# A relative-bias table kept in DRAM: one reversed row per head in place of 128 copies, and the reads that follow from it

## What is computed

```
def dsa_attention(q, k, v, iq, ik, iw, rel_bias):
    ...
        sc = jax.nn.relu(jnp.einsum('bthd,bsd->bths', iqb, ik))
        score = jnp.einsum('bths,bth->bts', sc, iwb).astype(jnp.float32)
        ...
        _, idx = lax.top_k(score, topk)
        ...
        bucket = t5_bucket(jnp.maximum(t[None, :, None] - idx, 0))
        bias = rel_bias[bucket].astype(jnp.float32).transpose(0, 1, 3, 2)
        logits = jnp.einsum('bthd,btkhd->bthk', qb, k_sel).astype(jnp.float32) * (dh ** -0.5) + bias
```

## Time and profile before

| | us |
|---|---|
| median of 3 runs | 1810.75 |
| lowest and highest run | 1805.5 and 1813.46 |
| span of the profiled execution | 1806.1 |
| PE busy | 1744.1 (97%) |
| DVE busy | 1028.2 (57%) |
| ACT busy | 854.6 (47%) |
| POOL busy | 628.9 (35%) |
| mean granted TensorE clock | 0.968 |

### The profile page before, as it was taken

The page is one execution under the profiler, slowest core; times in us unless marked ns, Lnnn a source line. Parts: engine busy times, 40 slices in busy tenths (PEclk is TensorE's granted clock), DMA queues, the critical chain, the costliest instruction groups (busy, mean ns, idle before and its releaser), DMA issues.

```text
span 1806.1 us, 23068 instructions
## 1 busy us (share of the span) xinstructions
PE 1744.1 (97%) x8072; PEld 1370.1 (76%) x8091; DVE 1028.2 (57%) x1633; ACT 854.6 (47%) x1366; POOL 628.9 (35%) x275
## 2 busy tenths in 40 slices
PE   7999999999999999999998999999999999999999
PEld 5548877767688778866667887888878788888887
DVE  4129937866733677677778325555547555556300
ACT  4222347665524455576664336676673343444220
POOL 3204421132244234443434432222124334444442
PEclk9759999999999899999999998999999999999999
DMA  6503222121323223311111321111113322333331
GB/s 180 126 12 94 94 88 59 42 81 48 127 86 111 69 72 104 95 57 47 48 47 49 111 74 47 48 47 47 48 48 105 94 82 93 93 100 97 95 103 59
DMA packets 40850, 141.16 MB, mean 78 GB/s; under 512 B 4664, under 2 KB 5144, under 8 KB 40632
## 3 DMA queue, kind: packets, MB, share of 16 engines
q1 hardware_dynamic: 37600, 131.96, 23.4%
q10 hardware_dynamic: 3160, 7.99, 2.1%
HBM read 135.21 MB, written 4.72 MB: 77 GB/s over the span
## 4 chain that ended last, share of the span: by engine, by line
PE 77%; DVE 11%; ACT 6%; issue 4%; DMA 1%; POOL 1%; DVEq 0%; POOLq 0%; ACTq 0%; SPq 0%
PE bank L673 15%; PE bank L675 14%; PE bank L674 14%; PE bank L1222 4%; PE bank L1223 4%; PE bank L1224 4%; PE bank L764 2%; PE bank L1117 2%; PE bank L724 1%; PE bank L726 1%; PE bank L725 1%; DMA w_raw<-weights 1%; PE bank L793 1%; PE bank L1136 1%; PE bank L1048 1%
## 5 line engine op out<-in xcount | busy, mean ns | idle before, releaser
L563 POOL TENSOR_TENSOR w_lo<-w_raw,w_hi 128x1024 fp32r<-128x1024 f32 x243 | 591.3, 2435 | 1138.8 <-ACT w_hi L1240 994.3
L673 PE MATMUL bank<-u_hi,w_hi 128*128 128x512 f32 x800 | 344.6, 431 | 3.2 <-DVE taps L2176 3.2
L675 PE MATMUL bank<-u_hi,w_lo 128*128 128x512 f32 x800 | 319.4, 399 | 0.0
L674 PE MATMUL bank<-u_lo,w_hi 128*128 128x512 f32 x800 | 318.9, 399 | 0.0
L1240 ACT ACTIVATE w_hi<-w_raw 128x1024 fp32r<-128x1024 f32 x199 | 209.3, 1056 | 227.1 <-PE bank L675 176.3
L673 PEld LDWEIGHTS bank<-u_hi,w_hi 128*128 128x128 f32 x800 | 153.7, 192 | 81.9 <-issue 49.4
L675 PEld LDWEIGHTS bank<-u_hi,w_lo 128*128 128x128 f32 x800 | 154.1, 193 | 33.9
L674 PEld LDWEIGHTS bank<-u_lo,w_hi 128*128 128x128 f32 x800 | 154.7, 193 | 28.5 <-issue 3.4
L1224 PE MATMUL bank<-u_hi,w_lo 128*128 128x512 f32 x320 | 124.6, 389 | 0.0
L1222 PE MATMUL bank<-u_hi,w_hi 128*128 128x512 f32 x320 | 124.6, 389 | 0.0
L1223 PE MATMUL bank<-u_lo,w_hi 128*128 128x512 f32 x320 | 124.6, 389 | 0.0
(11 more groups left out here) (444 smaller groups left out, 3637.4 us busy)
## 6 DMA issues: line engine op xcount, KB each, us to landing
w_raw<-weights SPq DMA_DIRECT2D x243, 512.0 KB, 3.5
bias_dram<-bias_row ACTq DMA_DIRECT2D x1, 2560.0 KB
xt<-x_t SPq DMA_DIRECT2D x8, 256.0 KB, 5.3
hank<-bias_dram ACTq DMA_DIRECT2D x8, 256.0 KB, 2.7
xt<-x_t ACTq DMA_DIRECT2D x1, 2048.0 KB, 9.5
out<-h_res SPq DMA_DIRECT2D x8, 256.0 KB
p_val<-p_t ACTq DMA_DIRECT2D x1, 512.0 KB, 11.6
trig<-trig ACTq DMA_DIRECT2D x1, 256.0 KB, 2.6
```

The costliest lines, as they stand in the source:

```text
L563: pool.tensor_tensor(w_lo[:, j, :], w_raw[:, j, :], w_hi[:, j, :].bitcast(F32), ALU.subtract).then_inc(w_lo_ready, 1)
L673: pe.matmul(o, hi, xh, start=(i == 0), stop=False)
L674: pe.matmul(o, hi, xl, start=False, stop=False)
L675: mm = pe.matmul(o, lo, xh, start=False, stop=(i == n - 1))
```

## The change

The table in DRAM becomes 8 rows of 640 values (20 KB) in place of 8 x 128 rows (2560 KB). The row is written backwards: ACT reads the two banks in the other order and each from its end. With a reversed row, partition p of the skewed tile begins p + 1 elements into the row, so that the load needs only positive steps: 128 overlapping rows of 2 KB, all out of the same 2560 bytes. The tile arrives mirrored, and DVE reads its first W columns from the last to the first. Instructions, their order on each engine, their number, the semaphores and the sizes of the loads of `hank` stay as they are.

```
-        bias_dram = nc.dram_tensor("bias_dram", (AH, P, HANK), F32).ap()
+        bias_dram = nc.dram_tensor("bias_dram", (AH, HANK), F32).ap()
...
-                ins = act.mul(bias_row[:, j * w:(j + 1) * w], bank[6 + j][0:AH, 0:w], ADH ** 0.5)
+                ins = act.mul(bias_row[:, j * w:(j + 1) * w], bank[7 - j][0:AH, 0:w][:, ::-1], ADH ** 0.5)
                 ins.then_inc(bias_out, 1)
             act.wait_ge(bias_out, 2)
 
-            rows = bias_row[:, :].unsqueeze(1).broadcast_to([AH, P, HANK])
-            act.dma_start(bias_dram, rows).then_inc(stored, 16)
+            act.dma_start(bias_dram, bias_row[:, :]).then_inc(stored, 16)
...
-                src = bass.AP(bias_dram.tensor, h * P * HANK + P - 1, [[HANK - 1, P], [1, S]])
+                src = bass.AP(bias_dram.tensor, h * HANK + 1, [[1, P], [1, S]])
                 act.dma_start(hank[:, h % 2, :], src).then_inc(hank_in[h % 2], 16)
...
-                dve.tensor_tensor(biased[:, n % 2, 0:W], hank[:, h % 2, S - W:S], chosen[:, ti, 0:W],
+                dve.tensor_tensor(biased[:, n % 2, 0:W], hank[:, h % 2, 0:W][:, ::-1], chosen[:, ti, 0:W],
                                   ALU.add).then_inc(da_bias, 1)
```

## The result

The changed kernel takes 1776.32 us (median of 4 runs, 1772.04 to 1778.86), the kernel before 1808.12 us beside it (4 runs, 1803.68 to 1813.46): a ratio of 0.9825, 95% interval 0.9805 to 0.9844. It is faster by 31.8 us. The forecast was 1777.7 us, 33.0 less than the 1810.75 us that the kernel before had then taken.

The account below looks back on a forecast made before the run. PE, busy 97% of the span, was taken to bound the kernel, at half clock in the indexer stage. Stage 32.6 us (stall included) plus 0.4 behind it: 33.0 off 1810.75 gives 1777.7 us, range 1768 to 1797.

Parts of the forecast that it names:

- The store takes the DMA engines from the loads, and the loads return to 3.5 us: Ahead of the indexer stage: the store shrinks from 344 to 2.7 engine-us, so weight loads land in about 3.5 us.
- the loads stay late: Rival: something other than the store holds the weight loads ahead of the indexer stage; 1811 us, chance 3%.
- Turns row by row: Part of that rival: store and loads alternate on the engines, so the store adds only 2.7 us to a load.
- The stall goes: PE's 2.14 us wait for ACT's relu before the third indexer step goes; already contained in the 33.0 us.
- The clock stays up through the stage: Indexer stage at the 2.4 GHz level: 41.7 us in place of 74.27, saving 32.6 us.
- The clock row: Granted clock's one dip, 45 to 135 us, traced to PE's gap before the third indexer step.
- What follows moves as a whole: From 134.92 us on all moves with the end of the scores; 0.4 us more from half clock behind the stage.
- `hank` and the backward reads at nothing: `hank` loads land in 2.7 us, with 9.03 us available, and DVE's backward additions cost no more; nothing counted.
- The gap of the earlier trace: A PE gap of 1.81 us elsewhere, followed by no clock fall; cited against the rival that the clock falls anyway.

Follow-up runs that it names:

- copy within DRAM: Kernel before, its 128-fold table made by a small store and a DRAM to DRAM copy, forward reads kept: 1769.88 us; again beside the changed kernel, 1775.98 us.
- three copies: Changed kernel with three linked ACT copies (about 1.9 us) in front of the first indexer relu: 1770.12, 1780.23 and 1805.23 us.
- five copies: Changed kernel with five linked ACT copies (3.2 us) in front of the first indexer relu: 1808.99 us.
- burst: Kernel before with 16 unneeded matmuls of 512 columns on PE behind indexer step 4: 1781.06 us.
- 96 copies: Changed kernel with each reversed row stored 96 times (1920 KB), tiles read from one copy: 1810.11 us.
- 128 copies: Changed kernel with only the store undone, the reversed row stored 128 times (2560 KB), backward reads kept: 1805.92 us.

## Why the prediction was right, step by step

- *The store takes the DMA engines from the loads, and the loads return to 3.5 us.* Right: 3.5 us in the median. The rival "the loads stay late" is out: with the store gone, or made otherwise, they are not late. The traces bear out the 8 engines: never more than 8 rows of the store are in flight, and alone on the queues (34 to 38 us) it takes 0.47 of the 16 engines for 51 GB/s. What a load loses beside it was argued too simply. Turns row by row were priced at 2.7 us a load; the loss is 15.7 us (19.2 against 3.5). How the engines divide their time between the two queues stays open. The copy within DRAM does not settle it either: row size, number of engines and the source all changed with it.
- *The stall goes.* Right, with the 1 us to spare that was worked out; three copies of 1.9 us made a gap of 0.90. That the loads land "15 us and more" before ACT wants them holds for the two late ones of the earlier trace rows, not for the first: issued at 37.99 it lands at 41.5, and ACT splits it at 50.81.
- *The clock stays up through the stage.* Right: 41.60 us against 41.7 forecast, steps of 1.52, 1.73 and 1.94 against 1.52, 1.74 and 1.95. The clock row too was taken from the right place: the gap by itself does it (five copies), and a stage that has lost it can hold it again (burst).
- *What follows moves as a whole.* Right: of the span's 33.5 us 32.7 lie in the stage. It starts 0.73 us later than before (61.38 against 60.65), so some 1.5 us were won behind it, where 0.4 were forecast. No experiment is about that rest. The profile of before has some 5 us more at half clock behind the stage than that of after, worth some 2.5 us; where such stretches fall differs from one trace to the next.
- *`hank` and the backward reads at nothing.* The reads were right to the nanosecond. The landing was off by 0.3 to 0.4 us, far inside the 9.03 us.
- *Details off:* 16 packets on ACT's queue in place of 8 (the 8 rows and 8 of 4 bytes), `hank` at 3.0 to 4.1 us where "under 3" was written. Neither is on the path. The DMA share from 35 to 85 us fell from 0.61 to 0.27, as forecast (0.25).
- *A forecast that was right with a reason put too simply.* The gap's effect was argued as if a gap of a given length had one outcome. The program with a gap of 0.9 us in its profile had times of both kinds, and 1.81 us did nothing at one place and cost 33 us at another (96 copies). The gap of the earlier trace rows was the one example picked; the same trace has the 2.31 us ahead of the attention stage, with a fall, which the prediction did not use. Nor is it the place: before one and the same matmul (L673, waiting for DVE; at 945.99 and 945.10 us) PE has a gap of 3.01 us both in the changed kernel and in the one with three copies; the mean clock from 946 to 950 us is 0.69 in the first and 1.00 in the second. And the moment of the fall moves: at the third step it came from 0.7 us before the gap's end (128 copies) to 1.7 us behind it (burst). What decides it besides the length stays open. It also makes the forecast a statement on the median: one of 13 executions of the kernel before ran as fast as the changed one (none of the 11 and 9 in the later sessions).

## What to carry to other kernels

A PE that is 97% busy can still have 2% to give: read the granted clock beside "busy", and where it is low for long, look for the first gap ahead of it and for what holds the waiting engine's program, not for the engine with most work. A large transfer is not paid by its bytes but by whom it makes late at one point: half of it was free, three quarters cost all, and all of it was free 70 us later. In a stage whose mix does not win the clock back, a gap of about 2 us cost 33 us here, so such a stage wants slack ahead of it, or a dense burst within. And where one execution in a dozen goes the other way, take several before you compare.

## What was not expected of the hardware

- The same program can end 30 us apart: 1775.98 us once in 13 executions of the kernel before against 1807.81 in the median, 1775.92 once in 4 with 128 copies, and 1770.12, 1780.23 and 1805.23 us with three copies in front of the first relu.
- 16 superfluous matmuls of 512 columns (4.66 us) made the kernel 27 us faster.
- A gap of 3.01 us before one and the same instruction was followed by a fall of the clock in one kernel's trace and by none in another's (0.69 and 1.00 from 946 to 950 us).
- Six reads of 128 overlapping 2 KB rows out of 2560 bytes take 3.0 us each in the median instead of 2.7: reading one small region 128 times cost next to nothing.
